# Hybrid feed-forward: high weights multiply the high and the low tokens in one 512-column product

## The reference, cut to what matters

```python
def hybrid_layer(x, positions, norm_g, w_in, ..., w_out, w_ff1, w_ff2):
    ...
    x = x + rms_norm(mixed, norm_g[1])
    hf = rms_norm(x, norm_g[2])
    ff = jnp.square(jax.nn.relu(hf @ w_ff1)) @ w_ff2
    return x + rms_norm(ff, norm_g[3])
```

## Time and profile before

| | us |
|---|---|
| median of 3 runs | 2252.05 |
| lowest, highest | 2248.34, 2257.75 |
| the profiled execution's own time | 2249.79 |
| its span, first to last instruction | 2248.1 |
| TensorE busy in the span | 2137.4 (95%) |
| VectorE busy in the span | 1087.9 (48%) |
| ScalarE busy in the span | 613.4 (27%) |
| mean granted clock of TensorE | 0.990 of full speed |

### The profile page before, as it was taken

One profiled execution on the slowest core, in us unless ns is written; L12 is line 12 of the kernel. 1 busy time (PEld: TensorE's weight loads), 2 busy tenths in 40 slices (PEclk: granted clock), 3 DMA queues, 4 the chain that ended last, 5 costly groups with the idle time before them and its releaser, 6 DMA issues.

```text
span 2248.1 us, 32119 instructions
## 1 busy us (share of the span) xinstructions
PE 2137.4 (95%) x12440; PEld 1388.0 (62%) x12440; DVE 1087.9 (48%) x1969; ACT 613.4 (27%) x1214; POOL 12.7 (1%) x20
## 2 busy tenths in 40 slices
PE   7999999999999889889999999999999999999998
PEld 4744644444343347564444444478989989898997
DVE  5677541111111136642222222167888777787876
ACT  4446532112121114431111111133451012434001
POOL 0000000000000010000000000000000000000000
PEclk9999999999999999999999999999999999999999
DMA  8189169998999994229999999952345546235452
GB/s 349 76 360 427 75 253 378 386 383 352 429 392 429 428 386 184 113 91 384 427 429 429 428 429 428 427 243 104 140 170 187 187 153 255 110 114 206 181 190 98
DMA packets 50146, 629.97 MB, mean 280 GB/s; under 512 B 5888, under 2 KB 6912, under 8 KB 11904
## 3 DMA queue, kind: packets, MB, share of 16 engines
q1 hardware_dynamic: 45008, 611.30, 66.7%
q10 hardware_dynamic: 2880, 9.44, 1.0%
q0 software_dynamic: 2160, 7.87, 0.9%
HBM read 614.42 MB, written 14.16 MB: 280 GB/s over the span
## 4 chain that ended last, share of the span: by engine, by line
PE 71%; DMA 15%; DVE 10%; ACT 2%; issue 2%; SPq 1%; DVEq 0%; ACTq 0%
PE ps L1908 10%; DMA ring<-in_ex_gate 7%; PE ps L1847 7%; DMA ring<-in_ex_up 6%; PE ps L1376 6%; PE ps L1378 6%; PE ps L1377 6%; PE ps L1987 4%; PE ps L1989 4%; PE ps L1988 4%; PE ps L1924 3%; PE ps L1803 3%; PE ps L1881 2%; PE ps L1723 1%; PE ps L1399 1%
## 5 line engine op out<-in xcount | busy, mean ns | idle before, releaser
L1908 PE MATMUL ps<-ring,E 128*64 128x512 f32 x1152 | 260.1, 609 | 16.7 <-DMA ring<-in_ex_up 14.4
L1378 PE MATMUL ps<-hn_hi,w_lo 128*128 128x256 f32 x928 | 262.4, 283 | 0.0
L1847 PE MATMUL ps<-ring,E 128*64 128x512 f32 x992 | 221.1, 598 | 10.5 <-DMA ring<-in_ex_gate 7.5
L1908 PEld LDWEIGHTS ps<-ring,E 128*64 128x64 f32 x1152 | 87.9, 140 | 185.6 <-issue 185.6
L2736 DVE TENSOR_TENSOR E<-E,ps 128x512 f32<-128x512 f32 x18 | 12.4, 688 | 354.3 <-PE ps L1908 354.3
L1378 PEld LDWEIGHTS ps<-hn_hi,w_lo 128*128 128x128 f32 x928 | 177.8, 192 | 0.0
L1847 PEld LDWEIGHTS ps<-ring,E 128*64 128x64 f32 x992 | 73.8, 138 | 142.3 <-issue 142.1
L1102 ACT ACTIVATE hT<-ps 128x512 f32<-128x512 f32 x70 | 41.9, 599 | 370.1 <-PE ps L1803 370.1
L1376 PE MATMUL ps<-hn_hi,w_lo 128*128 128x256 f32 x480 | 138.3, 288 | 1.7 <-DVE w_lo L2838 1.7
L1377 PE MATMUL ps<-hn_lo,w_lo 128*128 128x256 f32 x480 | 135.7, 283 | 0.0
L2838 DVE TENSOR_TENSOR w_lo<-ring,w_hi 128x4096 fp32r<-128x4096 f32 x30 | 132.8, 4426 | 1.0
(11 more groups left out here) (557 smaller groups left out, 3847.0 us busy)
## 6 DMA issues: line engine op xcount, KB each, us to landing
ring<-in_ex_up SPq DMA_DIRECT2D x64, 2048.0 KB, 16.0
ring<-in_ex_gate SPq DMA_DIRECT2D x62, 2048.0 KB, 16.6
ring<-in_ex_down SPq DMA_DIRECT2D x60, 2048.0 KB, 14.8
ring<-in_w_layer SPq DMA_DIRECT2D x56, 2048.0 KB, 8.2
ring<-in_w_static SPq DMA_DIRECT2D x33, 2048.0 KB, 17.0
y_rows<-E ACTq DMA_DIRECT2D x36, 256.0 KB, 8.4
ring<-in_ex_down SPq DMA_DIRECT2D x8, 1024.0 KB, 16.2
E<-in_w_layer SPq DMA_DIRECT2D x2, 2048.0 KB, 13.0
```

Of the source, the lines that this page charges most:

```text
L1378: return pe.matmul(out, lo, xhi, start=False, stop=last)
L1847: ins = pe.matmul(ps[half(u), 2 + w, :], xg[:, k, half(u)], weights, start=k == 0, stop=k == KC - 1)
L1908: ins = pe.matmul(ps[half(u), 2 + w, :], xg[:, k, half(u)], slab(2 * w + u, (KC, DE))[:, k, :], start=k == 0, stop=k == KC - 1)
```

## The change

`hn_hi` and `hn_lo` become the two planes of one tile, `hn_pair`, at the addresses at which they lay before. In hidden slabs 1 to 7 a step `k` is two products and no longer three: the high weights multiply both planes in one product of 2 x 256 columns, into both halves of the PSUM bank, and the low weights multiply the high tokens as before, onto the lower half. The bank then holds the sum in two halves. ScalarE copies the upper half to a free part of `sqb`, VectorE adds it to the lower half in PSUM, and the relu and scaling then read `sqb`, not PSUM. The counts of `ffh_ready` change since ScalarE now raises it twice a chunk.

```diff
--- before.py
+++ after.py
@@ -254,8 +254,9 @@
 
         w_hi = rounded("w_hi", [P, 2, SLAB], "E", 0)
         w_lo = [rounded(f"w_lo{r}", [P, SLAB], "ring", r * SLAB) for r in range(RING)]
-        hn_hi = rounded("hn_hi", [P, KC, NX], "ring", 5 * SLAB)
-        hn_lo = rounded("hn_lo", [P, KC, NX], "hT", 0)
+        hn_pair = rounded("hn_pair", [P, 2, (address["hT"] - address["ring"]) // 4 - 5 * SLAB], "ring", 5 * SLAB)
+        hn_hi = hn_pair[:, 0, 0:KC * NX].rearrange("p (k t) -> p k t", k=KC)
+        hn_lo = hn_pair[:, 1, 0:KC * NX].rearrange("p (k t) -> p k t", k=KC)
         ff_hi = rounded("ff_hi", [P, 8, NX], "xT", KC * NX)
         ff_lo = rounded("ff_lo", [P, 8, NX], "cat", 4 * 512)
         onsa_hi = rounded("onsa_hi", [P, 4, NX], "cat", 0)
@@ -600,6 +601,9 @@
             return (g, (KC, DE)), (u, (KC, DE)), (d, (EC, D))
 
 
+        def low_copied(i, m):
+            return 32 + 60 * i + 4 + 2 * (m - 4) + 1
+
         @block.sync
         def _(sp):
             sp.dma_start(par[:, 0:par_head], params_in[:, 0:par_head]).then_inc(inputs_in, 16)
@@ -1331,6 +1335,8 @@
                     act.wait_ge(ht_mm, TURNED0 + 2 * i + b + 1)
                     act.activation(ff_hi[:, 0:4, b * P:b * P + P], ps[:, 1 + b, :].rearrange("p (c t) -> p c t", c=4), ACT.Copy).then_inc(rt_ev, 1)
                 for m in range(4, FF // P):
+                    act.wait_ge(f1_mm, 32 * i + m + 1)
+                    act.activation(sqb[:, m % 4, NX:2 * NX], ps[:, 4 + m % 4, NX:2 * NX], ACT.Copy).then_inc(ffh_ready, 1)
                     act.wait_ge(f1_ev, 32 * i + m + 1)
                     r = sqb[:, m % 4, 0:NX]
                     act.activation(r, r, ACT.Square).then_inc(ffh_ready, 1)
@@ -1376,6 +1382,12 @@
                 pe.matmul(out, hi, xhi, start=first, stop=False)
                 pe.matmul(out, hi, xlo, start=False, stop=False)
                 return pe.matmul(out, lo, xhi, start=False, stop=last)
+
+            def three_pair(out, hi, lo, pair, k, nk):
+
+                both = pair[:, :, k * NX:k * NX + NX]
+                pe.matmul(out.rearrange("p (a t) -> p a t", a=2), hi, both, start=k == 0, stop=False)
+                return pe.matmul(out[:, 0:NX], lo, both[:, 0, :], start=False, stop=k == nk - 1)
 
             def mm_chunk(out, w, m0, rhs, nk=KC, start=True, stop=True):
                 for k in range(nk):
@@ -2222,7 +2234,7 @@
                     ins.then_inc(f1_mm, 2)
 
                 def turn_hidden(b):
-                    pe.wait_ge(ffh_ready, 32 + 32 * i + 2 * b + 2)
+                    pe.wait_ge(ffh_ready, 32 + 60 * i + 2 * b + 2)
                     for c in range(4):
                         ins = pe.transpose(ps[:, 1 + b, c * P:c * P + P], sqb[:, b, c * P:c * P + P], ident)
                     ins.then_inc(ht_mm, 1)
@@ -2235,8 +2247,7 @@
                     hi, lo = take(i, J_FF + n)
 
                     def part(c, k):
-                        return three(ps[:, 4 + c, 0:NX], hi[:, k, c * P:c * P + P], lo[:, k, c * P:c * P + P], hn_hi[:, k, :], hn_lo[:, k, :],
-                                     k == 0, k == KC - 1)
+                        return three_pair(ps[:, 4 + c, :], hi[:, k, c * P:c * P + P], lo[:, k, c * P:c * P + P], hn_pair, k, KC)
 
                     for c in range(4):
                         pe.wait_ge(f1_ev, 32 * i + 4 * j + c - 3)
@@ -3030,11 +3041,14 @@
                         for c in range(5):
                             m = 4 * j + c
                             if c < 4:
+                                r, low = sqb[:, m % 4, 0:NX], sqb[:, m % 4, NX:2 * NX]
                                 dve.wait_ge(f1_mm, 32 * i + m + 1)
-                                dve.scalar_tensor_tensor(sqb[:, m % 4, 0:NX], ps[:, 4 + m % 4, 0:NX], 0.0, rB, ALU.max, ALU.mult).then_inc(f1_ev, 1)
+                                dve.wait_ge(ffh_ready, low_copied(i, m))
+                                link(dve.tensor_tensor(r, ps[:, 4 + m % 4, 0:NX], low, ALU.add))
+                                dve.scalar_tensor_tensor(r, r, 0.0, rB, ALU.max, ALU.mult).then_inc(f1_ev, 1)
                             if c >= 1:
                                 m -= 1
-                                dve.wait_ge(ffh_ready, 32 + 32 * i + m + 1)
+                                dve.wait_ge(ffh_ready, low_copied(i, m) + 1)
                                 parts(ff_hi[:, m % 8, :], ff_lo[:, m % 8, :], sqb[:, m % 4, 0:NX]).then_inc(ffs_ready, 1)
                     if n + 2 < len(FF_ORDER):
                         split_both(i, J_FF + n + 2)
```

## The result

| | before | after |
|---|---|---|
| median, 20 runs each | 2254.34 us | 2260.26 us |
| lowest to highest | 2247.61 to 2258.06 | 2255.95 to 2265.55 |
| span of the profiled execution | 2248.1 | 2254.2 |

The ratio is 1.003 with a 95% interval of 1.0021 to 1.004: 5 to 9 us slower. In medians of 20 runs each the difference is 5.9 us, in the two profiled executions 6.1.

A forecast was written before the change was run, and what follows sets the result against it. TensorE was taken to set the time. Its gain of 6.0 us, partly lost to late splits at layer ends, netted +2.3 us; a clock drop added 3.4: +5.8, median 2257.8 us, range 2246 to 2267.

The forecast's parts named there:

- Who bounds what: Whole kernel: TensorE sets the time except at each layer's start and end, where it waits for VectorE's split.
- The round trip: VectorE and ScalarE, hidden slab chunks: addition, relu, square, copy in turn take 1.65 us a chunk, 7.09 for four, against 4.22.
- Start of a layer: Before hidden slab 2: VectorE's split comes late, so TensorE starts at 1715.29 against 1712.63, 2.66 us later.
- The clock: Behind the new stop before hidden slab 2: TensorE's clock drops for a while, 1.7 us a layer, 3.4 in all.
- The steady cycles: Hidden slabs 2 to 6: later splits stay hidden, each slab keeps its 0.43 us gain, 2.15 us a layer.
- The end of a layer: Before output slab 7: thinner cover, only 36 products between, so it begins 20.94 us after hidden slab 7, 0.66 later.
- The cover of the cycle: Steady cycle: split ready at 20.94 us, TensorE back at 21.99, leaving 1.05 us of cover.
- the slower rival: Hidden slabs 2 to 6: the round trip bounds the loop, next slab waits for its split; 2266.9 or 2286.5 us; 13 in 100.
- What a measurement can tell: Whole kernel: a change of 0.5%, 11.3 us, is about what a measurement can tell from none.

The follow-up runs named there:

- The run with the nearer columns: Changed kernel with the wide product's 512 columns from two neighbouring high-token chunks, not two planes; single run, hidden slab 11.29 us, stretches 158.83 and 158.84 us.

## Why the prediction was right, and where it wasn't

Forecast were +5.8 us (the terms themselves add up to 5.7), measured 5.9 in medians. Which engine waits for which and where, and which way the time moves, came out as forecast. That the two numbers lie so close is partly luck: term by term the profile has 2.4 us more in the two stretches, nearly all of it from one term, and the unchanged rest of the program, in these two profiles, gives 2.0 of them back.

- *Who bounds what.* Right. TensorE is bound by VectorE's split at the two ends of a layer and nowhere between. Undoing TensorE's part left both stops, undoing the others' part removed the first and left the second as short as before the change.
- *The round trip.* 7.09 us forecast for four chunks, 7.26 measured; 1.65 us a chunk, 1.70 to 1.72 measured; the idle time ahead of the second addition 0.8 forecast, 0.82 measured. The bounds by the nearest rows held: an addition of PSUM and SBUF takes 0.42 us and ScalarE's copy 0.36 to 0.39.
- *Start of a layer.* 2.66 us later forecast, 2.77 measured, counted from hidden slab 1 (26.51 against 23.74).
- *The clock.* 1.7 us forecast, 1.49 measured in this profile, and 0.1 to 2.9 in others with a stop as long: a cost that comes on some stops and not on others. To take it in was right, to take it as certain wasn't.
- *The steady cycles.* Here a term was mis-sized. I took 0.0133 us a step; a step fell by 0.007 only (0.22 us a hidden slab of 32 steps), because a product of 512 columns in turn with one of 256 takes 0.236 and not 0.227 us. The neighbouring rows I had read were products of one width in a row. Five cycles gave 1.0 us a layer instead of 2.15; beside the step it is the output slab, which takes 10.94 us in them and not 10.91. The rule of the Trainium skill that I had set beside the rows ("TensorE: Matmul & The Clock Gate", "Back-to-back issue gap") would by my estimate have left 1.1 of the 6.0 us. The Trainium skill gives it there for a single product by itself, which I hadn't said, and for a stream of weight loads and products it has 131 ns at 512 columns; the rows have 227, and they decide. The measured 0.22 us x 14 slabs = 3.1 us lies between that rule's gain and mine.
- *The end of a layer.* 0.66 us forecast, 0.80 measured (21.08 from hidden slab 7 to output slab 7, before 20.28). The size came out right, the reason didn't carry it: I had VectorE behind by its round trips, but with the trips cut by the order the split began only 0.08 us sooner, because the last chunk's own way is as long.
- *The cover of the cycle,* 1.05 us, was computed as one path's and is really VectorE's idle time, 1.57. This changed nothing in the forecast and put the slower rival too near.
- *What a measurement can tell.* I took 0.5% for that; with 20 runs each the interval of the ratio is 0.1% to either side, and 0.3% stands clear of it.

The sum a layer: 2.66 + 1.7 - 2.15 + 0.66 = 2.87 forecast, 2.77 + 1.49 - 0.99 + 0.80 = 4.07 measured, 8.1 us for both. That the medians give 5.9 has two readings that I can't part: the interval of the ratio reaches to 9 us and holds 8.1, and if the clock doesn't fall in every run, 5 is the cost without it and 8 that with it. The run with the nearer columns shows that both happen; how often, no run here shows.

## What to carry to other kernels

A gain of a few nanoseconds a product is paid for on the engines that feed it: count what each chunk adds to the engine that is due next, and look for the places where that engine has no idle time, here the first and the last slab of a layer. Check a gain in busy time where the change is: the total can move as much by itself. When two engines hand a chunk back and forth, the order on the idle one decides: moving its copy ahead of its square cut the time from VectorE's first addition to its split from 7.3 us to 5.8, and moving work that isn't due behind the work that is took it to 3.3, which, with the widths grouped, turned a loss of 0.3% into a gain of 0.2 to 0.3%.

## What the hardware did that I had not expected

- A float32r product of 512 columns takes 0.227 us in an output slab, 0.230 in a hidden slab with the widths grouped, and 0.236 in turn with one of 256; the pair takes 0.353 us, and 0.348 where the widths are grouped.
- Two planes of the moving operand cost no more than one piece (11.29 us a slab in both).
- At stops of 2.7 us and more before hidden slab 2, TensorE's granted clock fell to 1.2 GHz in eight cases of ten, in some before TensorE resumed and in some up to 1.4 us after it; at 1.2 us it fell in none of two. With products that filled the stop it stayed up in all four layers, but they must be cheap: a float32 product of 256 columns takes 0.42 us and a float32r one 0.12.
